# Turning normalised tiles by transposing DMAs instead of TensorE, and issuing the first transfers ahead of the parity branch, in a hybrid decoder block on eight cores

## The reference

```python
h = rmsnorm(x, norm_mix_g)                       # over the 1024 features
q, f, i, g, c_gate, b_gate, xb, gate_a, gate_b = split(h @ w_in)
y_a = hgrn2_mixer(q, f, i, g, ...) @ w_branch_a  # S_t = diag(f_t) S_{t-1} + k_t v_t^T, carried along the sequence
y_b = (b_gate * causal_conv3(c_gate * xb)) @ w_branch_b
x = x + (sigmoid(gate_a) * y_a + sigmoid(gate_b) * y_b) @ w_out
h2 = rmsnorm(x, norm_ffn_g)
x = x + (silu(h2 @ w_gate) * (h2 @ w_up)) @ w_down   # inner width 2816
out = rmsnorm(x, norm_final_g)
```

## Time and profile before

| | |
|---|---|
| three runs, slowest core | 1014.77, 1015.64, 1016.02 us (median 1015.64) |
| the profiled execution | 1016.44 us |
| its slowest core, core 4 (even) | span 1014.9 us |
| spans of the even cores 0, 2, 4, 6 | 1011.2, 1010.7, 1014.9, 1011.0 us |
| spans of the odd cores 1, 3, 5, 7 | 1011.2, 1012.0, 1009.9, 1009.5 us |
| core 4: TensorE, VectorE, ScalarE busy | 974.9, 435.5, 376.3 us |

### The profile page before, as it was taken

How to read it: one execution, slowest core, us unless ns; L and a number is a source line. 1 busy time by engine, 2 the same in 40 slices (tenths; PEclk the granted TensorE clock), 3 DMA queues, 4 the chain that set the end, 5 groups by cost and what they waited for, 6 DMA issues and landing times.

```text
span 1014.9 us, 15424 instructions; the slowest of 8 cores (1009.5 to 1014.9 us)
## 1 busy us (share of the span) xinstructions
PE 974.9 (96%) x5574; PEld 526.6 (52%) x5574; DVE 435.5 (43%) x678; ACT 376.3 (37%) x668; POOL 24.6 (2%) x52
## 2 busy tenths in 40 slices
PE   0889999999999999999999999999999999999997
PEld 0435646455556554455555645555464655444455
DVE  3535467776877664566544212122221212223223
ACT  3434285948586742445534111111111111111112
POOL 2000000000000000000000000000000000000000
PEclk9999999999999999999999999999999999999999
DMA  6982405100003544334387040203003053323112
GB/s 125 237 199 46 79 1 94 33 1 2 1 1 55 113 97 112 116 119 140 124 176 150 1 84 1 43 1 64 21 5 79 2 125 125 125 106 119 63 63 59
DMA packets 18947, 78.74 MB, mean 78 GB/s; under 512 B 2224, under 2 KB 2224, under 8 KB 15792
## 3 DMA queue, kind: packets, MB, share of 16 engines
q0 software_dynamic: 6336, 33.03, 18.5%
q1 hardware_dynamic: 12393, 44.38, 13.2%
q10 hardware_dynamic: 135, 0.25, 0.1%
HBM read 93.05 MB, written 17.63 MB: 109 GB/s over the span
## 4 chain that ended last, share of the span: by engine, by line
PE 90%; DMA 4%; ACT 2%; issue 2%; DVE 1%; SPq 1%; POOL 0%; ACTq 0%; DVEq 0%; POOLq 0%
PE pf L830 60%; PE pf L1454 16%; PE pf L841 10%; DMA ring<-wall 3%; DMA ring<-xall 1%; ACT arena L806 1%; PE pf L859 1%; PE pf L1079 1%; SPq L747 0%; ACT L806 0%; PE pf L1254 0%; PE pf L1256 0%; PE pf L1215 0%; PE pf L1234 0%; PE pf L1304 0%
## 5 line engine op out<-in xcount | busy, mean ns | idle before, releaser
L830 PE MATMUL pf<-hT,ring 128*128 128x384 bf16 (+2 forms) x3200 | 607.8, 346 | 6.4 <-DMA ring<-wall 3.2
L830 PEld LDWEIGHTS pf<-hT,ring 128*128 128x128 bf16 x3200 | 311.9, 98 | 273.2 <-issue 11.3
L1454 PE MATMUL pf<-ring,arena 128*128 128x512 bf16 (+2 forms) x735 | 159.8, 373 | 0.0
L806 ACT ACTIVATE rtmp<-pf 128x512 f32<-128x512 f32 (+2 forms) x114 | 59.9, 531 | 203.2 <-PE pf L830 196.5
L1454 PEld LDWEIGHTS pf<-ring,arena 128*128 128x128 bf16 (+1 forms) x735 | 76.2, 105 | 78.1
L810 DVE TENSOR_TENSOR arena<-rtmp,pf 128x512 bf16<-128x512 f32 (+2 forms) x85 | 51.7, 609 | 143.1 <-PE pf L830 129.5
L806 ACT ACTIVATE arena<-pf 128x512 f32<-128x512 f32 (+11 forms) x145 | 77.7, 572 | 75.5 <-PE pf L830 68.8
L830 PE MATMUL pf<-arena,ring 128*128 128x512 bf16 (+2 forms) x320 | 70.8, 345 | 1.5 <-ACT arena L806 1.4
L806 ACT ACTIVATE rtmp<-hT 128x1024 bf16<-128x1024 f32 (+3 forms) x19 | 18.4, 967 | 130.7 <-DVE hT L810 130.7
L841 PE MATMUL pf<-ring,hT 128*128 128x512 bf16 (+1 forms) x272 | 62.6, 379 | 0.0
L806 ACT ACT_TABLE_LOAD x44 | 56.5, 1283 | 6.6 <-DVE sso L1262 3.7
(11 more groups left out here) (101 smaller groups left out, 572.9 us busy)
## 6 DMA issues: line engine op xcount, KB each, us to landing
ring<-wall POOLq DMA_DIRECT2D x24, 1024.0 KB, 11.4
ring<-xall SPq DMA_DIRECT2D x14, 512.0 KB, 8.7
arena<-xall SPq DMA_DIRECT2D x14, 512.0 KB, 4.4
x1spill<-arena SPq DMA_DIRECT2D x14, 512.0 KB, 3.0
hT<-x1spill SPq DMA_DIRECT2D x14, 512.0 KB, 4.4
out<-hT SPq DMA_DIRECT2D x14, 512.0 KB, 2.6
ring<-wall POOLq DMA_DIRECT2D x12, 256.0 KB, 10.6
ring<-wall POOLq DMA_DIRECT2D x6, 512.0 KB, 5.8
```

The source lines that it names most:

```text
L806: P.op("act", lambda E: E.activation(out=rs(out), in_=rs(in_), func=func, **kw), reads=reads, writes=writes, dur=dur, aset=ASET[func] if f ...
L830: last = E.matmul(pb(bk)[:, 0:ncol], lhsT=sl[:, o_:o_ + 128], rhs=rhs[:, c, :], start=(c == 0), stop=(c == kc - 1))
L1454: last = E.matmul(pb(bk)[0:CH, 0:w], lhsT=act_v(c)[:, r0:r0 + CH], rhs=rl[c], start=(c == 0), stop=(c == 21))
```

## The change

(a) `dma_transp`: an SP-queue DMA turns the scaled tile from SBUF straight into `hT`, and VectorE multiplies `hT` in place. It replaces `transp` in the first norm from tile 8 (even) or tile 15 (odd, counted over the tiles of both passes) on and in the second norm everywhere, where the tile's width is a multiple of 16. (b) The last blocks change: 3 tiles of 124 tokens on even cores and in the odd cores' first pass, 4 tiles of 100 on odd cores. (c) The x loads 0 to 3, the constants and the first eight quarter-slab loads are issued before the branch; the weights are laid out in load order so that both programs name the same slab. (d) The gate constants are computed after the first norm's first block. (e) The planner's choice of PSUM banks changes (`strict` for even cores), and the odd program merges `conv_gen` with `pf_gen`, `pt_gen`, `pv_gen`. (f) `act` is placed by block.

```diff
-BL_EVEN = [(4, 128), (4, 128), (3, 128), (3, 128), (3, 120)]
-BL_ODD = [(4, 128), (4, 128), (4, 128), (4, 102)]
+BL_EVEN = [(4, 128), (4, 128), (3, 128), (3, 128), (3, 124)]
+BL_ODD = [(4, 128), (4, 128), (4, 128), (4, 100)]
...
+    def mark(self):
+        self.pre = [o.i for o in self.ops if o.eng in ("sp", "pool")]
+        for i in self.pre:
+            self.ops[i].prio = i - 1e6
...
-    def schedule(self, nbanks, window=48, hold=6.0):
+    def schedule(self, nbanks, strict, window=48, hold=6.0):
...
-                t = max(bank_free[k:k + n])
-                if best is None or t < best[0]:
-                    best = (t, k)
-            return best
+                if strict and not oldest:
+                    rest = [h or k <= j < k + n for j, h in enumerate(held)]
+                    if not any(not rest[j] and not rest[j + 1] for j in range(0, nbanks, 2)):
+                        continue
+                key = (not strict and n == 1 and not held[k ^ 1] and not oldest, max(bank_free[k:k + n]))
+                if best is None or key < best[0]:
+                    best = (key, k)
+            return None if best is None else (best[0][1], best[1])
...
     def run(E, e):
+        known = {}
+        odd.run(E, e, known, 0)
         pid = E.partition_id()
         with E.If(pid & 1):
-            odd.run(E, e)
+            odd.run(E, e, dict(known), 1)
         with E.Else():
-            even.run(E, e)
+            even.run(E, e, dict(known), 1)
...
         load_next([None, None, xm[0], xm[1]], 4)
         load_next([xm[1], xm[2], xm[3], xm[3]], 4)
+        P.mark()
...
+        def dma_transp(xs, b_xs, gcol, dst, b_dst, t, w):
+            out = dst[:, :, t * w:(t + 1) * w]
+            P.dma("sp", lambda E: E.dma_start_transpose(out=out, in_=xs), reads=[b_xs], writes=b_dst, chan=cyc("dtr", ch_tr),
+                  nbytes=524288)
+            tt(out, out, cst[:, gcol:gcol + 8].rearrange("p (c o) -> p c o", o=1).to_broadcast([128, 8, w]), ALU.mult,
+               b_dst + [b_cst], b_dst)
...
+        FIRST_DMA = 15 if odd else 8
...
+                turn = dma_transp if n >= FIRST_DMA and w % 16 == 0 else transp
                 if pend is not None:
-                    transp(xs1[pend[0]][0:w, :], b_xs1[pend[0]], G1, dst, b_dst(pend[1]), pend[1], w)
+                    turn(xs1[pend[0]][0:w, :], b_xs1[pend[0]], G1, dst, b_dst(pend[1]), pend[1], w)
...
-                        transp(xs_[0:CH, :], b_xs, G2, hTs[b], [b_hT[b][tm]], tm, CH)
+                        (dma_transp if CH % 16 == 0 else transp)(xs_[0:CH, :], b_xs, G2, hTs[b], [b_hT[b][tm]], tm, CH)
...
             drain(npre(0))
+            gate_consts()
...
-            merge((seq(halo_gen(), conv_gen(0, P1S)), 26.0), (npre(3), 2.5))
-            merge((seq(pf_gen(3), pt_gen(2), pv_gen(3)), 16.2), (norm_gen(hTs[1], mn(1)), 2.5))
-            merge((conv_gen(1, P1S), 23.4), (npre(4), 2.5))
-            merge((seq(pf_gen(4), pt_gen(3), pv_gen(4)), 16.2), (norm_gen(hTs[2], mn(2)), 2.5))
-            merge((conv_gen(2, P1S), 23.4), (norm_gen(hTs[3], mn(3)), 2.5), (pt_gen(4), 2.5))
+            merge((seq(halo_gen(), conv_gen(0, P1S)), 26.0), (seq(npre(3), norm_gen(hTs[1], mn(1))), 5.0))
+            merge((conv_gen(1, P1S), 23.4), (seq(pf_gen(3), pt_gen(2), pv_gen(3)), 12.5), (seq(npre(4), norm_gen(hTs[2], mn(2))), 5.0))
+            merge((conv_gen(2, P1S), 23.4), (seq(pf_gen(4), pt_gen(3), pv_gen(4)), 12.5), (norm_gen(hTs[3], mn(3)), 2.5))
+            drain(pt_gen(4))
...
-        P.schedule(8)
+        P.schedule(8, not odd)
```

More of the change, by code:

```diff
@@ L122, in __init__ @@
         self.lead = 0
+        self.pre = []
         for e in ENGS:
@@ L201, in schedule @@
         left = len(ops)
+        pre_left = {e: sum(1 for i in self.pre if ops[i].eng == e) for e in ENGS}
+        pre_set = set(self.pre)
         for o in ops:
@@ L226, in schedule @@
                 cand = sorted(avail[e], key=lambda i: ops[i].prio)[:window]
+                if e == "pe" and head_pe < len(pend_pe) and pend_pe[head_pe] in avail[e] and pend_pe[head_pe] not in cand:
+                    cand.append(pend_pe[head_pe])
+                if pre_left[e]:
+                    first = min(i for i in self.pre if ops[i].eng == e and ops[i].fin is None)
+                    cand = [i for i in cand if i == first]
                 rows = []
@@ L307, in number, with run @@
                     self.val[i] = ("P_" + e, n)
-    def run(self, E, e):
+    def run(self, E, e, known, part):
         ops, val = self.ops, self.val
-        known = {}
         own = "P_" + e
-        for i in self.order[e]:
+        npre = sum(1 for i in self.pre if ops[i].eng == e)
+        for i in self.order[e][:npre] if part == 0 else self.order[e][npre:]:
             o = ops[i]
@@ L330, in run @@
                 o.fn(E).then_inc(self.sems[own], 1)
-        if e == "sp":
+        if e == "sp" and part == 1:
             for b in self.finals:
@@ L341, in emit_both @@
     even.number()
+    assert odd.pre == even.pre
+    for i in odd.pre:
+        assert odd.val[i] == even.val[i] and odd.ops[i].deps == even.ops[i].deps
     def run(E, e):
+        known = {}
+        odd.run(E, e, known, 0)
         pid = E.partition_id()
         with E.If(pid & 1):
-            odd.run(E, e)
+            odd.run(E, e, dict(known), 1)
         with E.Else():
-            even.run(E, e)
+            even.run(E, e, dict(known), 1)
     @block.tensor
@@ L663, in pair, with act_v @@
             return tokpair(i)[0][:, 0:2 * T], pair_b[i, T]
[L665 to L674, removed]
+        act_off = {}
+        at = {"arena": 0, "misc": 0}
+        for j in range(22):
+            for b in range(NB):
+                sp = "arena" if at["arena"] + 2 * TB[b] <= ARENA else "misc"
+                act_off[j, b] = (sp, at[sp])
+                at[sp] += 2 * TB[b]
+        assert at["misc"] <= 6144
+        act_b = [[reg(f"act{j}_{b}", *act_off[j, b], 2 * TB[b]) for b in range(NB)] for j in range(22)]
+        def act_v(j, b):
+            sp, o_ = act_off[j, b]
+            return (arena if sp == "arena" else misc)[:, o_ // 2:o_ // 2 + TB[b]]
         c1s = []
@@ L1591 @@
     SLABS = slab_table()
-    wall = np.zeros((len(SLABS), 128, 4096), f32)
-    for i, parts in enumerate(SLABS.values()):
-        for kind, key, r0, kc, c0, nc_, off in parts:
-            w = W[key][r0:r0 + kc * 128, c0:c0 + nc_].reshape(kc, 128, nc_)
-            if kind == "rhs":
-                w = w.transpose(1, 0, 2)
-            else:
-                w = w.reshape(kc, 128, nc_ // 128, 128).transpose(1, 2, 0, 3)
-            wall[i, :, off:off + kc * nc_] = w.reshape(128, kc * nc_)
+    walls = {}
+    for odd in (True, False):
+        wall = np.zeros((len(SLABS), 128, 4096), f32)
+        for i, name in enumerate(LOADS[odd]):
+            for kind, key, r0, kc, c0, nc_, off in SLABS[name]:
+                w = W[key][r0:r0 + kc * 128, c0:c0 + nc_].reshape(kc, 128, nc_)
+                if kind == "rhs":
+                    w = w.transpose(1, 0, 2)
+                else:
+                    w = w.reshape(kc, 128, nc_ // 128, 128).transpose(1, 2, 0, 3)
+                wall[i, :, off:off + kc * nc_] = w.reshape(128, kc * nc_)
+        walls[odd] = wall
     in_maps = []
@@ L1609 @@
             xall[0:TOK_EVEN] = x[b, 0:TOK_EVEN]
-        in_maps.append({"xall": xall, "cst": cst, "gf": gf, "wall": wall})
+        in_maps.append({"xall": xall, "cst": cst, "gf": gf, "wall": walls[half == 1]})
     nc = _get_nc()
```

39 lines of the change are left out of this document (22 added, 17 removed).

## The result

| | before | after |
|---|---|---|
| median of the runs shown together | 1015.2 us (4 runs, 1013.4 to 1016.02) | 1068.2 us (4 runs, 1055.32 to 1221.56) |
| the two runs of after that the ratio uses | | 1055.32 and 1057.05 us |
| even cores, mean of the four | 1010.5 us | 1052.4 and 1053.6 us |
| odd cores, mean of the four | 1009.7 us | 1010.0 and 1007.2 us |

The ratio is 1.0406, 95% interval [1.0377, 1.0435], with a forecast of 1010.7 us and a range of 1000 to 1021. In some executions cores came out late at a lower clock, and the ratios and the means over even and odd cores leave these executions out while the medians do not. A mean for before is the median over the runs made beside the experiments.

What follows compares the result with a forecast made beforehand. PE was taken as the bound, with even core 4 deciding: 1014.9 - 10.5 - 9.0 + 3.6 + 2 + 6.0 + 3 = 1010.0 us of span, giving a forecast of 1010.7 us, range 1000 to 1021.

Steps and rivals of the forecast that it cites:

- transfers ahead of the branch: Start of even cores: first x loads issued 8.8 us earlier, 10.5 us won on core 4, 7.2 on core 0.
- columns and rows of 124 tokens: Feature-major and convolution matmuls of even cores' last block: 12 more columns in 716 matmuls cost 3.6 us.
- four-engine transfers: 124-row transfers use 4 DMA engines: 6.0 us more at the last stores, 3 us of PE time in d_gen.
- second norm by DMAs: Even cores' second norm: 14 tiles no longer turned on PE, 0.45 us won for each.
- first norm by DMAs: Even cores' first norm: tiles 8 to 13 no longer turned on PE, 0.45 us won for each.
- The transposing DMA: Both norms: DVE waits for late landings; 2 us lost, bounds zero and 62 us, one landing at worst 10.3 us.
- a cover of 6.4 us: DVE can stand about 6.4 us before PE loses time, read from core 5's wait for an x tile.
- rival C: Transposing DMA becomes the wait; 1031 us, slower than before from an average landing of about 10.5 us; chance 0.17.
- E: Rival: four-engine loads in d_gen stop PE for 10 us and delay slabs sharing the engines; 1018 us, chance 0.08.
- Odd cores: Odd program, reckoned from core 3: forecast at 998 us, far from the bound.
- the multiply at zero: VectorE's multiply takes 1218 ns from PSUM and 1221 SBUF to SBUF: no change in time.
- rival B: Narrow tiles cost nothing that shows, 11 us of the sum shrink to 2; 1001.5 us, chance 0.20.

Runs made afterwards that it cites:

- e3: Changed kernel with every tile turned on TensorE and the old widths (120 and 102 rows in the last blocks); 1013.93 us, ratio 1.0006.
- e6: Changed kernel with all tiles turned on TensorE and each 124-row transfer cut into 112 and 12 rows; 1012.71 us, ratio 0.9991.
- e2: Changed kernel with every tile turned on TensorE, 124 and 100 rows kept; 1037.44 us, ratio 1.0240.
- e4: Changed kernel with turning DMAs in the second norm alone, 124 and 100 rows kept; 1035.37 us, ratio 1.0210.
- e5: Changed kernel with turning DMAs in the second norm alone and the old widths (120 and 102 rows); 1010.3 us, ratio 0.9967.
- e8: Changed kernel with turning DMAs in the second norm alone and each 124-row transfer cut into 112 and 12 rows; 1007.96 us, ratio 0.9952.
- e9: Changed kernel with all turning DMAs kept and each 124-row transfer cut into 112 and 12 rows; 1020.52 us, ratio 1.0029.
- e11: Changed kernel with 124-row transfers cut into 112 and 12 and even cores' slabs f and i asked for after block 3's third tile; 1004.76 us, ratio 0.9913.
- m1: Separate kernel without the block's work: turns a 128x1024 tile alone, behind x loads, beside slab loads, or both, plus a plain copy; 537.91 us in all.

## Why the prediction was wrong, step by step

The even cores' mean went from 1010.5 to 1053.0 us. The chain of kernels before, e3, e6, e2, e4, after splits these 42.5 us by the prediction's own steps:

| step | forecast | measured on even cores |
|---|---|---|
| transfers ahead of the branch, planner (e3 - before) | -7.2 to -10.5 | -4.9 |
| columns and rows of 124 tokens (e6 - e3) | +3.6 | +4.4 |
| four-engine transfers (e2 - e6) | +6.0 and +3 | +21.5 |
| second norm by DMAs, 14 tiles (e4 - e2) | -6.3 | -0.8 (-5.0 in e5 - e3, -4.8 in e8 - e6) |
| first norm by DMAs, 6 tiles (after - e4) | -2.7 | +22.2 |
| what turning DMAs cost in all | +2 | in the two rows above |

**The transposing DMA** is the step that failed first. I had a landing of 10.3 us as the worst case for one, from spills beside slabs, and a cover of 6.4 us, and then took 2 us because "the slabs run beside only a few". Those few were the first of the six tiles of the first norm, and two of them were enough: tile 8's DMA landed after 23.6 us and tile 9's after 42.4, and since this kernel's DVE and SP work in a fixed order, PE stood 31.2 us on core 0. My bound was from one kind of traffic; the landing grew with two kinds that add, 12.3 and 9.5 us each and 20.1 together when measured alone. What I left out altogether is SP's own time for the issue. "Which has a tile's time in hand" was said of the x load behind it, and 9.3 us of issue took from that in `d_gen`. How much this cost is not shown: PE stood there for 14.8 us, but in e2, without any turning DMA, for 16.6; what is measured is that the second norm's turning gains 0.8 us beside uncut 124-row transfers and 5.0 or 4.8 without them. My measure for rival C, slower from an average landing of 10.5 us on, was wrong for the same reason: the 14 in the second norm had a median of 3.3, and two in the first decided.

**The four-engine term** was right in kind and too small. At the end SP waits 6.9 us (forecast 8.4, +4.6 instead of +6.0). In `d_gen` I scaled the wait from a 102-row load on six engines and took 3 us of PE time with a bound of 10; the load took 32 to 35 us and PE stood 14.8 to 16.6 (e2's are without any turning DMA). The cover of 6.4 us was not there either: DVE waited 15.2 us for the load and PE 14.8 behind it, 18.4 and 16.6 in e2, so 0.4 to 1.8 us were covered. "In the first norm these tiles have over 30 us in hand: zero" holds for the tiles and missed their neighbours, the turning DMAs behind them on the queue: 9.5 us to land there instead of 3.1 when measured alone. That they wait for their share of the same four engines fits this; no view shows it engine by engine.

**C and E came together.** I gave them 0.17 and 0.08 as cases that exclude each other, priced at 1031 and 1018. They met on SP's queue, and the range did not reach to both at once.

**The start** was over-priced. On core 4 the second x load went out at 2.01 us instead of 12.29, and yet PE's wait fell by 4.4 us on core 0 and 2.9 on core 4. I wrote that "ACT and DVE branch as before". The first instruction of ACT behind the branch stood at 7.34 us on core 0 before, and the first tile's statistics at 16.71, behind an x load. The timelines of ACT on core 0, before and with the change:

```profile
7.34 1.28 ACT L730 ACT_TABLE_LOAD   x1 [7.34 <-DVE e2l L784]
```

```profile
11.20 1.28 ACT L757 ACT_TABLE_LOAD   x1 [11.20 <-DVE e2l L814]
12.50 0.20 ACT L757 ACTIVATE zw<-zw 128x1 f32<-128x1 f32 x1
12.61 1.04 ACT L836 ACTIVATE arena<-ring 128x1024 bf16<-128x1024 f32 x1
```

x is there (ACT doesn't wait for the load any more), and ACT starts 3.9 us later than it did (13.12 against 7.90 on core 4). The bracket names DVE: ACT waits for DVE's first fills, and DVE's very first instruction, which waits for nothing in the profile, moved from 7.20 to 11.06 us (7.76 to 12.98 on core 4). DVE's way into the branch is now what the start waits for.

The trace's records of the packets that load instructions (queues q8 and q14 of the page) say more. Behind the start the first such packet on the even cores stood at 3.46 to 4.08 us before, and stands at 9.05 to 11.17 with the change; DVE's first instruction follows it by 2.8 to 3.7 us before and 2.0 to 3.3 after. The odd cores, which take the branch that lies first, have none by then. And from 2 to 10 us the DMA share of the even cores is 0.90 to 1.00 where it was 0.09 to 0.26. So the even program's instructions come late, and they come by DMA while the early transfers keep that share up. That the one causes the other fits all these figures; no run moved the transfers back alone.

**Odd cores** were forecast at 998; with the change they are at 1007 to 1010, since in their first pass they too load 124-row tiles and turn others behind them (core 5's PE waits 9.5 us at L1121). With the rows cut they are where I had them, 995.5 (e9) and 997.4 (e11). For them it is the two together that cost: the first norm's turning loses 6.7 us beside uncut rows (1001.9 in e4, 1008.6 with the change) and gains 6.6 beside cut ones (1002.1 in e8, 995.5 in e9), while e4 and e8 are alike. **Right** were the count and price of the PE work taken out (0.36 of 0.45 us a tile kept), the multiply at zero, the columns, and the rule that the number of DMA engines is the largest up to 16 that divides the rows: share 0.22 for 124 rows, and with 112 + 12 SP's wait at the end is 1.7 us instead of 6.9. The Trainium skill ("DMA: Bandwidth & Descriptors", why a DMA increments its semaphore by 16) states it, and e2 against e6 agrees. Its price for a transpose by DMA ("VectorE: DVE Perf Modes", the three transpose paths), an estimated 10.5 us for a tile, is three times the 3.1 measured alone; the sum went wrong by the traffic around it.

Two sums of the prediction are off by a little and change nothing: 8.4 - 2.3 is 6.1, and rival B's comes to 1001.7.

**Open.** Why an issue on SP takes 27 us: it goes with the two loads, the one ahead on its own queue above all, but what holds it no run tells. That the d_gen loss would be smaller with the x tiles asked for earlier was not tried. Nor was the later slab gate alone, without turning DMAs: e11's 4.2 us over e8 (even cores, 1005.3 to 1001.1) contain both it and the six tiles, forecast at 2.7.

## What to carry to other kernels

Before a transfer is put on a path that an in-order engine waits for, list what else those DMA engines carry at that very moment and price the worst single landing, not the average: a DMA that lands in 3 us alone took 42 behind 124-row loads and beside slab loads. Choose row counts that spread over 16 engines, or cut off the remainder: 112 + 12 rows instead of 124 gave back 21 us for one more instruction each. When two risks share a resource, give them a case of their own in which both happen.

## What the runs showed of the hardware

- The time that SP needs to issue a transposing DMA is not fixed: 1.2 us when quiet, 1.2 to 1.6 beside slab loads alone, 3 to 5 behind a 124-row load, 10 to 14 with slab loads as well (m1, all cores), up to 27.0 in the kernel.
- A 128x1024 bf16 tile turned SBUF to SBUF lands in 3.1 us, a plain copy of the same bytes under load only 2 us earlier than the turned one.
- With the transfers issued ahead of the branch, DVE's first instruction behind it came at 9.8 to 13.9 us on the even cores of the twelve kernels that have them, against 6.3 to 7.8 before, and at 3.0 to 4.7 on the odd cores, against 2.8. The first packets that load the even program's instructions came at 9.05 to 11.17 us in after, against 3.46 to 4.08.
- Even cores with first-norm turning beside slabs scatter (in e9 single ones reach 1021.8 us where others of the same run are at 1008 to 1012), those of e6 and e8, without it, stay within 4.2 us of each other. Why is not shown.
